# The first weight sum of each mix round: two fetches on GpSimd's queue in place of an add on VectorE

## The chip, the cores and the metric

One core of one Trainium2 chip runs the kernel. The metric is the device time of one execution in microseconds. A change of about 0.2% is what the timed runs of this kernel can tell from none.

## What is computed

One layer of a streaming encoder with sequence length S = 512 and model width D = 1024, all in float32. The part that matters here is the branch gates: three of them, each S x D, made from the normalised input and 3 x 1024 columns of w_in, then used to mix three branch results.

```python
h = rms_norm(x, attn_norm[l])
proj = h @ w_in[l]
q, k, v, f_logit, u, cv, cb, cc, g = jnp.split(proj, IN_SPLIT_POINTS, axis=-1)
...
y_a = forgetting_attention(...) @ w_proj_attn[l]
y_b = multiscale_pool(u, pool_w[l], pool_scale[l]) @ w_proj_pool[l]
y_c = short_gated_conv(cv, cb, cc, conv_w[l]) @ w_proj_conv[l]
gates = jax.nn.sigmoid(g + b_gate[l]).reshape(B, S, N_BRANCH, D)
mixed = gates[..., 0, :] * y_a + gates[..., 1, :] * y_b + gates[..., 2, :] * y_c
x = x + mixed @ w_out[l]
```

Then follow a SwiGLU block and a last norm.

## The kernel before

The kernel is written by hand, engine by engine, with semaphores between them. SyncE (SP) issues the loads, ScalarE rounds each weight block to a high part (whi), VectorE subtracts it to get the low part (wlo), and TensorE makes each product from three multiplies: high by high, high by low, low by high. TensorE takes float32 words of reduced precision at full speed, so each part is of that type. Weight blocks pass through rings: raw (three slots of 1024 columns, filled by SP), whi and wlo.

Its stages in order are norm, front, pair (four times), mix, rounds, out, ffn_first, ffn (three times), ffn_last and down. The change is in the rounds and in what prepares the first of them at the end of mix.

There are ten rounds (ROUNDS). Each makes two blocks of 128 gate columns of one branch, and the two blocks of that branch's projection. The gate product has a 2 x 2 block form: two column blocks by two halves of the model width (rows), and two halves of the tokens. It is computed in seven multiplications in place of eight, by sums of weight quarters and sums of token quarters. The weight quarters, each 128 x 512 in the tile, are b11 and b21 (load 0 of the round, first and second half of the rows for the first column block) and b12 and b22 (load 1, the same for the second block). Nine parts of weights go through the rings in a round: B11, B21, PRJ_A, T2, T1, T3, B22, PRJ_B, T4. TensorE works in this order: quarter products B11 and B21, projection PRJ_A, quarters T2, T1, T3, B22, projection PRJ_B, quarter T4. PRJ_A and PRJ_B are products of 128 x 512 tiles (lines 894 to 896), the quarters of 128 x 256 (lines 856 to 860).

The weight sums are made by sum_weights(r) on VectorE (lines 1840 to 1849), four adds of 128 x 512:

- weight_sum(0) = b11 + b12, the first sum, which becomes part T1
- b12 = b12 + b22, in place in raw, which becomes part T3
- weight_sum(1) = weight_sum(0) + b22, the second sum, part T2
- weight_sum(2) = weight_sum(1) + b21, the third sum, part T4

Each raises weight_summed by one, four a round. The three sums live in tail_32, a tile of 2,560 columns of which the token sums of the mix stage (chunk_whole, chunk_sums, chunk_lo; lines 1801 to 1824) use the first 2,048, until sums_lo_done reaches 4.

VectorE's own order in the loop over r is: post(r - 1) (gates times projections, L1880, and adds onto the merged branches, L1886), T3 and B22 low parts of round r, bank add c11 (L1906), PRJ_B, merged_lo (L1565) after a third branch, T4, then sum_weights(r + 1), bank add c12_first (L1914), B11 and B21 of round r + 1, bank adds c22 (L1921) and c12_second (L1929), and PRJ_A, T2 and T1 of round r + 1 (all low parts are L1855). In round 0 the parts B11 and B21 of round 1 stand ahead of sum_weights(1). ScalarE's order is alike: the high parts are L1250, the sigmoids L1289, the copies of banks L1274. In rounds 1 and up, the second gate's sigmoid stands between T2's and T1's high parts, and waits for the last bank add of the round.

SP's loads of a round (L535) wait until the ring slot is written out: load 0 for B21's low part of the round before and for all of its weight sums, load 1 for B22's low part, load 2 (two projection blocks) for PRJ_B's. Each load is two transfers of 256 KB, in rows of 128 elements of 4 bytes.

GpSimd makes constants at the start, issues 16 small copies within SBUF during the pair stage (L653, L655), and at the end of the kernel raises the variances to the power -0.5 (L663). Between the two it waits.

TensorE's waits in a round are: the low part of each quarter, kept (the bank copied by ScalarE), posted(4 r + 1) ahead of B22, and y_free ahead of the two projections, which post(r - 1) raises by its two multiplies.

Of the kernel before, what the change touches and what calls it, by code (L numbers as in the profile page):

```python
# [19 lines left out]
ALU = mybir.AluOpType  # L20
# [6 lines left out]
P = 128  # L27
# [11 lines left out]
ROUNDS = [(0, 2)] + [(i, br) for i in range(1, 4) for br in range(3)]  # L39
# [71 lines left out]
def hybrid_block(nc, x, attn_norm, w_in, b_forget, b_gate, w_proj_attn, pool_w, pool_scale,  # L111
# [3 lines left out]
    S, D = x.shape  # L115
# [22 lines left out]
    with ExitStack() as ctx:  # L138
# [3 lines left out]
        def sem(name):  # L142
            return ctx.enter_context(nc.semaphore(name))
# [167 lines left out]
        def weight_part(r, j):  # L311

            return PARTS_AT + PER_ROUND * r + j
# [14 lines left out]

        def weight_sum(j):

            return tail_32[:, j * HALF:(j + 1) * HALF]

        def gate_at(r, m):

# [89 lines left out]
        kept, posted, gates = sem("kept"), sem("posted"), sem("gates")  # L424
        y_free, merged = sem("y_free"), sem("merged")
        x_again = sem("x_again")

        def landed_down(k):

# [23 lines left out]
        def _(sp):  # L453
            def load(stage, i, j, halves, width=P):

                n, s = unit(stage, i, j)
                if stage == "out" and j < SLOTS:
                    sp.wait_ge(w_lo, weight_part(len(ROUNDS) - 1, (B21, B22, PRJ_B)[j]) + 1)
                    if j == 0:
                        sp.wait_ge(weight_summed, 4 * len(ROUNDS))  # L460
                    sp.sem_inc(loads_begun, 1)
                elif not (stage == "front" and n < SLOTS):
                    sp.wait_ge(w_lo, n - SLOTS + 1)


                    sp.sem_inc(loads_begun, 1)
                for src, at in halves:
                    nb = src.shape[0] // P
                    dst = raw[:, s, at * width:(at + nb) * width].rearrange(
                        "p (k c) -> p k c", c=width)  # L470
                    sp.dma_start(dst, src.rearrange("(k p) c -> p k c", p=P)
                                 ).then_inc(landed[s], 16)
# [65 lines left out]
            for r, (i, br) in enumerate(ROUNDS):  # L538
                if r == 0:
                    sp.wait_ge(w_lo, PARTS_AT - 2)  # L540
                else:
                    sp.wait_ge(w_lo, weight_part(r - 1, B21) + 1)
                    sp.wait_ge(weight_summed, 4 * r)
                load_round(r, 0, gate_columns(br, 2 * i))
                sp.wait_ge(w_lo, PARTS_AT - 1 if r == 0 else weight_part(r - 1, B22) + 1)
                load_round(r, 1, gate_columns(br, 2 * i + 1))
                sp.wait_ge(w_lo, PARTS_AT if r == 0 else weight_part(r - 1, PRJ_B) + 1)
                load_round(r, 2, projections((br, 2 * i), (br, 2 * i + 1)))
# [63 lines left out]
        @block.gpsimd  # L612
        def _(pool):
            nc.gpsimd.memset(ident[:], 0.0).then_inc(consts, 1)
            nc.gpsimd.memset(mask[:], 0.0).then_inc(consts, 1)
            nc.gpsimd.memset(ones[:], 1.0).then_inc(consts, 1)
            pool.wait_ge(consts, 3)
            nc.gpsimd.affine_select(out=ident[:], in_=ident[:], compare_op=ALU.not_equal, fill=1.0,
                                    base=0, pattern=[[-1, P]], channel_multiplier=1
                                    ).then_inc(consts, 1)  # L620
            nc.gpsimd.iota(steps16[:], pattern=[[1, PAD]], base=1, channel_multiplier=0
                           ).then_inc(consts, 1)

            diag = mask[:, S - P:S]
            nc.gpsimd.affine_select(out=diag, in_=diag, compare_op=ALU.is_ge, fill=NEG_INF,
                                    base=0, pattern=[[-1, P]], channel_multiplier=1
                                    ).then_inc(consts, 1)

            begun = 0
            for tiles, first, fill in ((Q2, 0, -1.0), (K2, 2, 1.0)):
                for a in range(2):
                    rows = op(tiles[a])
                    nc.gpsimd.memset(rows.bitcast(F32), 0.0).then_inc(f_consts, 1)
                    begun += 1
                    for r in (first, first + 1):
                        pool.wait_ge(f_consts, begun)
                        nc.gpsimd.affine_select(out=rows, in_=rows.bitcast(F32),
                                                compare_op=ALU.not_equal, fill=fill,  # L640
                                                base=-((1 - a) * HD + r), pattern=[[0, S]],
                                                channel_multiplier=1).then_inc(f_consts, 1)
                        begun += 1
            assert begun == F_CONSTS
            pool.wait_ge(f_consts, F_CONSTS)
            pool.wait_ge(vector_tile, count("vector_tile", "front", 0, 2))
            for i in range(WB):
                if i > 0:
                    pool.wait_ge(full[6], count("full6", "pair", i - 1, 2))
                for a in range(2):  # L650
                    h, at = 2 * i + a, (1 - a) * HD
                    f_pair = big_y[h:h + F_LOW + 1:F_LOW, F_AT:F_AT + S]
                    pool.dma_start(op(Q2[a], S, slice(at + 2, at + 4)).bitcast(F32), f_pair  # L653
                                   ).then_inc(f_in, 16)
                    pool.dma_start(op(K2[a], S, slice(at, at + 2)).bitcast(F32), f_pair  # L655
                                   ).then_inc(f_in, 16)


            nc.gpsimd.memset(stat[:, MINUS_HALF:MINUS_HALF + 1], -0.5).then_inc(power, 1)
            pool.wait_ge(power, 1)  # L660
            for t in range(TB):
                pool.wait_ge(x2_var, t + 1)
                nc.gpsimd.tensor_tensor(stat[:, 12 + t:13 + t], stat[:, 4 + t:5 + t],  # L663
                                        stat[:, MINUS_HALF:MINUS_HALF + 1], ALU.pow
                                        ).then_inc(x2_rstd, 1)
# [417 lines left out]
        def _(act):  # L1083
# [173 lines left out]

            def sum_hi(r, j, c, done):

                act.wait_ge(weight_summed, 4 * r + done)  # L1260
                part_hi(r, j, weight_sum(c))

            def t3_hi(r):

                act.wait_ge(weight_summed, 4 * r + 2)
                raw_hi(r, T3, 1, 0, 2)

            TOK = S // 2
# [56 lines left out]
            chunk_hi(1)  # L1325
            gate(4, 5, 3, 1, 1)
            raw_hi(0, PRJ_A, 2, 0)
            sum_hi(0, T2, 1, 3)
            sum_hi(0, T1, 0, 1)

            for r in range(len(ROUNDS)):
                last = r == len(ROUNDS) - 1
                if r > 0:
                    last_gate(r - 1)
                slots_free(r)
                keep(r, B11, 0, 0)
                t3_hi(r)
                raw_hi(r, PRJ_B, 2, 1)
                first_gate(r)
                if r > 0 and ROUNDS[r - 1][1] == 2:  # L1340
                    merged_hi(r - 1, 0)
                    merged_hi(r - 1, 1)
                keep(r, T2, 1, 0)
                sum_hi(r, T4, 2, 4)
                if last:
                    split_hi("out", 0, 0)
                    keep(r, T3, 1, 1)
                    split_hi("out", 0, 1)
                    second_gates(r)
                else:  # L1350
                    raw_hi(r + 1, B11, 0, 0, 2)
                    keep(r, T3, 1, 1)
                    raw_hi(r + 1, PRJ_A, 2, 0)
                    sum_hi(r + 1, T2, 1, 3)
                    if r == 0:
                        sum_hi(r + 1, T1, 0, 1)
                        second_gates(r)
                    else:
                        second_gates(r)
                        sum_hi(r + 1, T1, 0, 1)  # L1360
            last_gate(len(ROUNDS) - 1)
            merged_hi(len(ROUNDS) - 1, 0)
            merged_hi(len(ROUNDS) - 1, 1)
# [172 lines left out]
        def _(dve):  # L1536
# [291 lines left out]
            def sum_weights(r):  # L1828
# [8 lines left out]
                    dve.wait_ge(sums_lo_done, 4)  # L1837
                else:
                    dve.wait_ge(w_lo, weight_part(r - 1, T1) + 1)
                nc.vector.tensor_tensor(weight_sum(0), b11, b12, ALU.add  # L1840
                                        ).then_inc(weight_summed, 1)
                nc.vector.tensor_tensor(b12, b12, b22, ALU.add).then_inc(weight_summed, 1)
                dve.wait_ge(weight_summed, 4 * r + 1)
                nc.vector.tensor_tensor(weight_sum(1), weight_sum(0), b22, ALU.add
                                        ).then_inc(weight_summed, 1)
                dve.wait_ge(weight_summed, 4 * r + 3)
                if r > 0:
                    dve.wait_ge(w_lo, weight_part(r - 1, T4) + 1)
                nc.vector.tensor_tensor(weight_sum(2), weight_sum(1), b21, ALU.add
# [513 lines left out]
```

## Time and profile before

| what | value |
|---|---|
| timed runs | 797.62, 797.9 and 798.65 us, median 797.9 |
| the profiled execution | 797.29 us, span 795.1 us |
| mean granted clock of TensorE | 0.997 of full speed |
| TensorE busy | 778.7 us, 98% of the span |
| VectorE busy | 561.0 us, 71% |
| ScalarE busy | 362.3 us, 46% |
| GpSimd busy | 21.0 us, 3% |
| moved by DMA | 83.44 MB, mean 105 GB/s |

Busy times are of one profiled execution and are counted within its span; the time of that execution is 2.2 us longer than the span. The rounds lie between about 240 and 395 us. A start time in a row is counted from the start of the span. In views that show DMA shares as digits, each digit is the busy share of 16 engines in tenths, in one fortieth of the window.

### The profile page before, as it was taken

The page shows a single profiled execution, that of the slowest core. Times are in us where ns is not written, and L with a number is a line of the kernel's source. Part 1 is how long each engine was busy: PE and PEld are TensorE (multiplying, and loading weights), DVE is VectorE, ACT ScalarE, POOL GpSimd, SP SyncE. Part 2 cuts the span into 40 slices and gives each one's busy share as a digit, 9 for nine tenths or more (in the row PEclk, how much of TensorE's full clock was granted, in tenths as well). Part 3 has the DMA queues.
Part 4 walks back from the last instruction along what each step waited for, and adds up shares of the span by engine and source line. Part 5 has one row for each costly group of instructions (what it writes and reads, how often), then busy time and mean ns, then how long its engine had stood idle before and what let it go on. Part 6 is the DMA issues. An engine that isn't in the chain of part 4 may idle for free.

```text
span 795.1 us, 11564 instructions
## 1 busy us (share of the span) xinstructions
PE 778.7 (98%) x3931; PEld 663.3 (83%) x3931; DVE 561.0 (71%) x877; ACT 362.3 (46%) x604; POOL 21.0 (3%) x43
## 2 busy tenths in 40 slices
PE   5999999999999999999999999999999999999996
PEld 4878888888889999999988888888888888887885
DVE  7878686868798778777643465454445456799997
ACT  7265555656444555555433532222222223556554
POOL 4011010100000000000000000000000000000001
PEclk9999999999999999999999999999999999999998
DMA  7423232323234343343452133333323332353432
GB/s 226 121 77 97 54 98 61 82 70 84 67 95 106 98 115 100 87 120 94 147 193 84 54 110 102 87 98 106 106 84 101 106 93 93 131 183 110 148 104 106
DMA packets 129257, 83.44 MB, mean 105 GB/s; under 512 B 5484, under 2 KB 118180, under 8 KB 129220
## 3 DMA queue, kind: packets, MB, share of 16 engines
q1 hardware_dynamic: 128708, 82.89, 35.6%
q8 instruction: 22, 0.36, 0.2%
q0 software_dynamic: 512, 0.07, 0.1%
q14 instruction: 15, 0.12, 0.0%
HBM read 80.77 MB, written 2.10 MB: 104 GB/s over the span
## 4 chain that ended last, share of the span: by engine, by line
PE 93%; DVE 4%; DMA 1%; issue 1%; ACT 1%; SPq 0%; POOLq 0%; POOL 0%; ACTq 0%; DVEq 0%
PE bank L686 18%; PE bank L690 18%; PE bank L688 18%; PE bank L860 4%; PE bank L858 4%; PE bank L856 4%; PE bank L1028 3%; PE bank L1030 3%; PE bank L1029 3%; PE bank L894 2%; PE bank L895 2%; PE bank L896 2%; PE bank L938 2%; PE bank L940 2%; PE bank L942 2%; PE bank L800 1%
## 5 line engine op out<-in xcount | busy, mean ns | idle before, releaser
L686 PE MATMUL bank<-operands,whi 128*128 128x512 f32 x624 | 244.7, 392 | 1.0 <-DVE operands L1567 1.0
L690 PE MATMUL bank<-operands,wlo 128*128 128x512 f32 x624 | 243.1, 390 | 0.0
L688 PE MATMUL bank<-operands,whi 128*128 128x512 f32 x624 | 242.9, 389 | 0.0
L1558 DVE TENSOR_TENSOR wlo<-raw,whi 128x1024 fp32r<-128x1024 f32 x86 | 105.2, 1224 | 75.7 <-ACT whi L1092 74.0
L686 PEld LDWEIGHTS bank<-operands,whi 128*128 128x128 f32 x624 | 117.2, 188 | 25.4 <-DVE wlo L1558 1.5
L690 PEld LDWEIGHTS bank<-operands,wlo 128*128 128x128 f32 x624 | 117.1, 188 | 24.7
L688 PEld LDWEIGHTS bank<-operands,whi 128*128 128x128 f32 x624 | 117.2, 188 | 24.1 <-issue 0.2
L1092 ACT CAST whi<-raw 128x1024 fp32r<-128x1024 f32 x86 | 89.8, 1046 | 48.9 <-PE bank L690 25.0
L1098 ACT ACTIVATE work<-work 128x512 f32<-128x512 f32 (+1 forms) x24 | 15.2, 632 | 82.3 <-DVE work L2063 80.3
L860 PE MATMUL bank<-sums_hi,wlo 128*128 128x256 f32 x160 | 45.3, 283 | 0.0
L858 PE MATMUL bank<-sums_lo,whi 128*128 128x256 f32 x160 | 45.3, 283 | 0.0
L856 PE MATMUL bank<-sums_hi,whi 128*128 128x256 f32 x160 | 45.2, 283 | 0.0
L1855 DVE TENSOR_TENSOR wlo<-raw,whi 128x1024 fp32r<-128x1024 f32 (+1 forms) x40 | 38.1, 952 | 5.5 <-ACT whi L1250 5.5
L1030 PE MATMUL bank<-whi,operands 128*128 128x512 f32 (+1 forms) x97 | 37.5, 387 | 0.0
L1250 ACT CAST whi<-raw 128x1024 fp32r<-128x1024 f32 (+1 forms) x40 | 33.4, 837 | 8.6 <-PE bank L860 5.6
L2068 DVE TENSOR_TENSOR work<-bank,big_y 128x512 f32<-128x512 f32 x22 | 15.2, 691 | 31.1 <-PE bank L690 31.1
L1855 DVE TENSOR_TENSOR wlo<-tail,whi 128x512 fp32r<-128x512 f32 x30 | 20.5, 690 | 23.4 <-ACT whi L1250 23.4
L2063 DVE TENSOR_TENSOR work<-bank,big_y 128x512 f32<-128x512 f32 x22 | 15.1, 688 | 29.1 <-PE bank L690 24.1
L1029 PE MATMUL bank<-wlo,operands 128*128 128x512 f32 (+1 forms) x91 | 35.2, 387 | 0.0
L1028 PE MATMUL bank<-whi,operands 128*128 128x512 f32 (+1 forms) x91 | 35.2, 387 | 0.0
L860 PE MATMUL bank<-operands,wlo 128*128 128x256 f32 x120 | 34.0, 283 | 0.0
L858 PE MATMUL bank<-operands,whi 128*128 128x256 f32 x120 | 34.0, 283 | 0.0
(253 smaller groups left out, 1393.6 us busy)
## 6 DMA issues: line engine op xcount, KB each, us to landing
raw<-in_w_in_dram SPq DMA_DIRECT2D x106, 256.0 KB, 3.2
raw<-in_w_gate_up_dram SPq DMA_DIRECT2D x88, 256.0 KB, 3.2
raw<-in_w_down_dram SPq DMA_DIRECT2D x55, 256.0 KB, 2.8
big_x<-in_x_dram SPq DMA_DIRECT2D x8, 512.0 KB, 4.3
raw<-in_w_out_dram SPq DMA_DIRECT2D x16, 256.0 KB, 3.2
raw<-in_w_proj_attn_dram SPq DMA_DIRECT2D x8, 256.0 KB, 4.1
raw<-in_w_proj_pool_dram SPq DMA_DIRECT2D x8, 256.0 KB, 4.0
raw<-in_w_proj_conv_dram SPq DMA_DIRECT2D x8, 256.0 KB, 4.0
```

The source lines that it names most:

```text
L686: nc.tensor.matmul(banks[b][:, 0:width], whi[:, s, w], op(hi + k * S), start=a, stop=False)
L688: nc.tensor.matmul(banks[b][:, 0:width], whi[:, s, w], op(lo + k * S), start=False, stop=False)
L690: mm = nc.tensor.matmul(banks[b][:, 0:width], wlo[:, s, w], op(hi + k * S), start=False, stop=z)
L856: nc.tensor.matmul(to, wh[:, w], xh, start=first and k == 0, stop=False, skip_group_check=not first)
L858: nc.tensor.matmul(to, wh[:, w], xl, start=False, stop=False, skip_group_check=not first)
L860: mm = nc.tensor.matmul(to, wl[:, w], xh, start=False, stop=k == 3, skip_group_check=not first)
L1028: nc.tensor.matmul(to, h, wh, start=first, stop=False, skip_group_check=onto)
L1029: nc.tensor.matmul(to, h, wl, start=False, stop=False, skip_group_check=onto)
L1030: return nc.tensor.matmul(to, l, wh, start=False, stop=last, skip_group_check=onto)
L1092: nc.scalar.copy(whi[:, s, :], raw[:, s, :]).then_inc(w_hi, 1)
L1558: nc.vector.tensor_tensor(wlo[:, s, :], raw[:, s, :], whi[:, s, :].bitcast(F32), ALU.subtract).then_inc(w_lo, 1)
L1855: nc.vector.tensor_tensor(part_at(wlo, r, j, n), src, part_at(whi, r, j, n).bitcast(F32), ALU.subtract).then_inc(w_lo, n)
```

## The change

The first sum is taken from VectorE and made by DMA. GpSimd's queue issues two transfers for each round, both from w_in in HBM: the first writes b11 into weight_sum(0), the second, issued when the first has landed, adds b12 onto it. They raise a new semaphore, first_sum_in, by 16 each, 32 a round. The first of a round is issued when the tile of the first sum is free: for round 0 when the first half of the token sums has its low parts, later when T1's low part of the round before is written and its weight sums are all made. VectorE's second sum, and ScalarE's high part of T1, wait for first_sum_in in place of the first add. weight_summed counts three a round in place of four, and all who wait for it are renumbered. weight_sum(0) moves to the last 512 columns of tail_32, which the token sums don't use.

```diff
@@ weight_sum
-            return tail_32[:, j * HALF:(j + 1) * HALF]
+            at = (4, 1, 2)[j] * HALF
+            return tail_32[:, at:at + HALF]
@@ SP, load("out") and the round loads
-                        sp.wait_ge(weight_summed, 4 * len(ROUNDS))
+                        sp.wait_ge(weight_summed, 3 * len(ROUNDS))
-                    sp.wait_ge(weight_summed, 4 * r)
+                    sp.wait_ge(weight_summed, 3 * r)
@@ GpSimd, after the copies of the pair stage
+            for r, (i, br) in enumerate(ROUNDS):
+                if r == 0:
+                    pool.wait_ge(sums_lo_done, 2)
+                else:
+                    pool.wait_ge(w_lo, weight_part(r - 1, T1) + 1)
+                    pool.wait_ge(weight_summed, 3 * r)
+                for m, op_ in ((0, ALU.bypass), (1, ALU.add)):
+                    if m == 1:
+                        pool.wait_ge(first_sum_in, 32 * r + 16)
+                    col = COL_G + br * D + (2 * i + m) * P
+                    pool.dma_start(weight_sum(0).rearrange("p (k c) -> p k c", c=P),
+                                   w_in[0:4 * P, col:col + P].rearrange("(k p) c -> p k c", p=P),
+                                   accum_op=op_).then_inc(first_sum_in, 16)
@@ ScalarE
             def sum_hi(r, j, c, done):
-                act.wait_ge(weight_summed, 4 * r + done)
+                if done == 0:
+                    act.wait_ge(first_sum_in, 32 * r + 32)
+                else:
+                    act.wait_ge(weight_summed, 3 * r + done)
                 part_hi(r, j, weight_sum(c))
...
-                        sum_hi(r + 1, T1, 0, 1)
+                        sum_hi(r + 1, T1, 0, 0)
@@ VectorE, sum_weights
-                nc.vector.tensor_tensor(weight_sum(0), b11, b12, ALU.add
-                                        ).then_inc(weight_summed, 1)
                 nc.vector.tensor_tensor(b12, b12, b22, ALU.add).then_inc(weight_summed, 1)
-                dve.wait_ge(weight_summed, 4 * r + 1)
+                dve.wait_ge(first_sum_in, 32 * r + 32)
                 nc.vector.tensor_tensor(weight_sum(1), weight_sum(0), b22, ALU.add
                                         ).then_inc(weight_summed, 1)
-                dve.wait_ge(weight_summed, 4 * r + 3)
+                dve.wait_ge(weight_summed, 3 * r + 2)
```

## Rows read from the trace of the kernel before

**Rows 1.** The page: TensorE's busy time, GpSimd's DMA queue, shares of the chain.
```profile
PE 778.7 (98%) x3931; PEld 663.3 (83%) x3931; DVE 561.0 (71%) x877; ACT 362.3 (46%) x604; POOL 21.0 (3%) x43
...
q0 software_dynamic: 512, 0.07, 0.1%
...
PE 93%; DVE 4%; DMA 1%; issue 1%; ACT 1%; SPq 0%; POOLq 0%; POOL 0%; ACTq 0%; DVEq 0%
```

**Rows 2.** Busy time of each engine by stretch; one round's length.
```profile
core 0: us, PE busy (x) PEld busy (x) DVE busy (x) ACT busy (x) POOL busy (x), PEclk, DMA share, GB/s
...
301.80:317.40 15.60, 15.60 (x111) 14.62 (x110) 13.11 (x22) 8.79 (x16) 0.00 (x0) 1.00 0.39 104
```

**Rows 3.** Waits, 238 to 395 us, the longest in total: total, times, longest.
```profile
DVE wlo L1855 <- ACT whi L1250: 28.9, 24, 2.9
```

**Rows 4.** Timeline of VectorE, round 5's sums: start, duration, line, tiles, idle before.
```profile
301.84 0.69 DVE L1855 TENSOR_TENSOR wlo<-tail,whi 128x512 fp32r<-128x512 f32 x1 [0.29 <-ACT whi L1250]
...
311.16 0.68 DVE L1840 TENSOR_TENSOR tail<-raw 128x512 f32<-128x512 f32 x1
311.76 0.69 DVE L1842 TENSOR_TENSOR raw<-raw 128x512 f32<-128x512 f32 x1
312.36 0.69 DVE L1844 TENSOR_TENSOR tail<-tail,raw 128x512 f32<-128x512 f32 x1
...
314.03 1.22 DVE L1855 TENSOR_TENSOR wlo<-raw,whi 128x1024 fp32r<-128x1024 f32 x1
...
317.40 0.69 DVE L1855 TENSOR_TENSOR wlo<-tail,whi 128x512 fp32r<-128x512 f32 x1 [0.29 <-ACT whi L1250]
318.63 0.69 DVE L1880 TENSOR_TENSOR work<-bank,work 128x512 f32<-128x512 f32 x1 [0.54 <-ACT work L1289]
```

**Rows 5.** Timeline of VectorE, the same places in rounds 0, 1 and 2.
```profile
223.94 2.36 DVE L1824 TENSOR_TENSOR sums_lo<-tail,sums_hi 128x1024 fp32r<-128x1024 f32 x2
...
241.79 0.69 DVE L1855 TENSOR_TENSOR wlo<-tail,whi 128x512 fp32r<-128x512 f32 x1
...
252.40 0.69 DVE L1844 TENSOR_TENSOR tail<-tail,raw 128x512 f32<-128x512 f32 x1
...
255.32 1.29 DVE L1855 TENSOR_TENSOR wlo<-tail,whi 128x512 fp32r<-128x512 f32 x2
...
265.68 0.69 DVE L1844 TENSOR_TENSOR tail<-tail,raw 128x512 f32<-128x512 f32 x1
```

**Rows 6.** Timeline of TensorE: first multiplies of B11 and PRJ_A, round 5.
```profile
317.92 0.28 PE L856 MATMUL bank<-operands,whi 128*128 128x256 f32 x1
...
320.80 0.40 PE L894 MATMUL bank<-operands,whi 128*128 128x512 f32 x1
```

**Rows 7.** Timeline of ScalarE after round 5's last bank add: the second gate's sigmoid.
```profile
315.94 0.73 ACT L1289 ACTIVATE work<-work,vecs 128x512 f32<-128x512 f32 x1 [1.32 <-DVE work L1929]
```

**Rows 8.** DMA issues of lines 655 (GpSimd) and 535 (SP): ns; then landings.
```profile
L655 POOL DMA_DIRECT2D operands<-big_y x8: 540/540/546, 54.1 to 146.6; - x8
...
DMA to landing us min/median/max: 1.6/1.6/1.7
...
L535 SPq DMA_DIRECT2D raw<-in_w_in_dram x36: 367/438/510, 241.3 to 369.5; - x36
...
DMA to landing us min/median/max: 2.9/3.4/6.1
```

**Rows 9.** DMA view of 306.5 to 312.5 us, four loads of a round.
```profile
DMA  0000000006936599999999999999999999821000
...
DMA packets 2112, 1.05 MB, mean 175 GB/s; under 512 B 64, under 2 KB 2112, under 8 KB 2112
```

**Rows 10.** DMA view of 302.6 to 312.4 us.
```profile
DMA  9600000000000000000004758999999999999410
```

**Rows 11.** VectorE's groups from 243 to 393 us: first and last of 16.
```profile
L1855 DVE TENSOR_TENSOR wlo<-raw,whi 128x1024 fp32r<-128x1024 f32 (+1 forms) x38 | 36.2, 952 | 5.5 <-ACT whi L1250 5.5
...
L1868 DVE TENSOR_TENSOR work<-work 128x512 f32<-128x512 f32 x1 | 0.7, 692 | 0.1
```

More of the change, by code:

```diff
@@ L426, in hybrid_block @@
         x_again = sem("x_again")
+        first_sum_in = sem("first_sum_in")
         def landed_down(k):
@@ L1258, in sum_hi @@
             def sum_hi(r, j, c, done):
-                act.wait_ge(weight_summed, 4 * r + done)
+                if done == 0:
+                    act.wait_ge(first_sum_in, 32 * r + 32)
+                else:
+                    act.wait_ge(weight_summed, 3 * r + done)
                 part_hi(r, j, weight_sum(c))
             def t3_hi(r):
-                act.wait_ge(weight_summed, 4 * r + 2)
+                act.wait_ge(weight_summed, 3 * r + 1)
                 raw_hi(r, T3, 1, 0, 2)
@@ L1327, in _ @@
             raw_hi(0, PRJ_A, 2, 0)
-            sum_hi(0, T2, 1, 3)
-            sum_hi(0, T1, 0, 1)
+            sum_hi(0, T2, 1, 2)
+            sum_hi(0, T1, 0, 0)
             for r in range(len(ROUNDS)):
@@ L1343, in _ @@
                 keep(r, T2, 1, 0)
-                sum_hi(r, T4, 2, 4)
+                sum_hi(r, T4, 2, 3)
                 if last:
@@ L1353, in _ @@
                     raw_hi(r + 1, PRJ_A, 2, 0)
-                    sum_hi(r + 1, T2, 1, 3)
+                    sum_hi(r + 1, T2, 1, 2)
                     if r == 0:
-                        sum_hi(r + 1, T1, 0, 1)
+                        sum_hi(r + 1, T1, 0, 0)
                         second_gates(r)
@@ L1359, in _ @@
                         second_gates(r)
-                        sum_hi(r + 1, T1, 0, 1)
+                        sum_hi(r + 1, T1, 0, 0)
             last_gate(len(ROUNDS) - 1)
```

## The prediction

> **What bounds the kernel now.** I read the page first. TensorE is busy 98% of the span and carries 93% of the chain that ended last [rows 1], so a change pays only where TensorE waits. The busy times by stretch then show the rounds, the stage the change is in: in a 15.6 us stretch TensorE is busy for all 15.60 us at the full granted clock (2.4 GHz), while VectorE works 13.1 us [rows 2]. The list of waits from 238 to 395 us has rows for VectorE and ScalarE as the waiting engines only, the longest of 28.9 us [rows 3]; none names TensorE as the waiting engine. So no time can be won in the rounds; the question is only whether the new path stays inside its margins.
>
> Those come from VectorE's order of time. A round takes (312.36 - 265.68) / 3 = 15.56 us [rows 4, 5]. Take round 5. Its weight sums are four adds of 0.6 us each: the first sum at 311.16 (the removed one), b12 + b22 at 311.76, the second sum, which reads the first, at 312.36, the third behind it. Then come B11's low part (ends 314.03 + 1.22 = 315.25), the bank adds, and T2's and T1's low parts, the last ending at 317.40 + 0.69 = 318.09 [rows 4].
>
> **What is removed.** Ten adds of 0.68 us (about 0.60 from start to start), all on VectorE under a busy TensorE [rows 2, 4]: worth 0, and this cover is gone only where TensorE would wait for VectorE. Time stays saved only if VectorE's next instructions came earlier and something waited for them. The second sum now waits for the fetch, and TensorE wants B11(5) only at 317.92 [rows 6], 2.67 us after it is ready.
>
> **What is added: a wait with a deadline.** The first sum of round r now comes from two fetches of 256 KB on GpSimd's queue, one after the other, each waited for. The first may start once T1's low part of round r - 1 is written, since ScalarE and VectorE still read the tile until then; the weight_summed count is met earlier. Call D the time from there to the second fetch landed. For round 5 the start is 301.84 + 0.69 = 302.53 and the old second sum began at 312.36: D up to 9.83 us keeps the old schedule, and the same holds for rounds 3 to 9. Round 1 has 252.40 - (241.79 + 0.69) = 9.92, round 2 has 265.68 - (255.32 + 1.29) = 9.07 [rows 5]. Round 0 starts after the first half of the token sums at 226.30 and has 13.5 us, not in question [rows 5].
>
> Behind VectorE's new wait stand sums two and three, B11, three bank adds, PRJ_A, T2, T1 and, in the next round, the post of the gates. From second sum to T1's end VectorE takes 318.09 - 312.36 = 5.73 us, including the detour through ScalarE (the gate's sigmoid waits for the last bank add, T1's cast stands behind it) [rows 4, 7]. So the new path is a loop: T1's end, D, 5.73 us, T1's end. It fits the period if D + 5.73 is at most 15.56. Where it doesn't, the lateness adds up round by round, and TensorE is hit when it exceeds the slack. The tightest use is the post: PRJ_A(5) starts at 320.80 [rows 6] and needs its first multiply, ended at 318.63 + 0.69 = 319.32 [rows 4], so 1.5 us to spare, plus 0.54 us that VectorE idled before it [rows 4]: 2.0 us. B11 has 2.67. Hence, with D over the margins, loss = (D - 9.92) + (D - 9.07) + 7 x (D - 9.83) - 2.0, where a first term below zero counts nothing. It is 0.2 us at D = 10.0, 1.5 at 10.15, 9.2 at 11, 18 at 12, 36 at 14.
>
> **How long is D?** The trace has no fetch of this size on GpSimd's queue and no adding one. From below: GpSimd's 4 KB copies land 1.6 us after issue [rows 8]; 256 KB more cost the engines a quarter of what four such loads took them [rows 9]: the digits of that row add up to some 23.5 slices of 0.15 us, 3.5 us, so 0.88 us a load; a fetch is then 2.5 us and two are 5.0. From above: GpSimd's 16 copies made 512 packets [rows 1], 32 each, in 0.54 us of its time, 17 ns a packet if all of it scaled; one load has 2112 / 4 = 528 packets [rows 9], so 8.9 us each plus 1.1 us to landing, D = 20 for both. I take neither: SP's loads have the same bytes, rows and source, and land in 2.9 to 6.1 us, median 3.4 [rows 8]. GpSimd's issue of 0.54 us against SP's 0.44 makes that 3.5 us for the first fetch, which meets idle engines: they rest from 303.1 to 307.7 us (slices of 0.245 us) [rows 10].
>
> The second fetch begins about 302.6 + 3.5 = 306.1. It must read the tile, add and write back; I cost that at two passes of the engines, 1.75 us instead of 0.88. And it collides: SP's next four transfers reach the engines at 307.7 [rows 10] and keep them full until 311.6 [rows 9]. Sharing them halves its rate, so from 307.6 (I allow 1.5 us from its issue to full speed, of the 2.9 that SP's shortest landing takes with 0.88 of moving [rows 8]) it takes up to 3.5 us, and 0.5 us to report: landed about 311.6, a leg of 5.5 us. D = 3.5 + 5.5 + 0.1 for the queue to wake = 9.1 us, inside 10.15 by 1.0 us and level with round 2's 9.07 (an overrun there of some tenths is within the 2.0).
>
> The Trainium skill (DMA: Bandwidth & Descriptors, Anatomy of one DMA) puts a GpSimd fetch at 2.0 us plus bytes over 436 GB/s; by it, as an estimate, two are 5.2 us. SP's loads here land at 2.9 us at best, above that, so the sum doesn't go by it. Collectives: The Full Stack (The bandwidth ceiling) says a reducing transfer runs at about half rate because it reads two sources; this agrees with my two passes, and no row here shows it.
>
> **The other parties.** SP's loads share the engines with the second fetch and may land up to 1.7 us later. b12 and b22 are in the first half of the four transfers that keep the engines busy from 307.7 to 311.6 [rows 9, 10], so they land at about 310.6, and are first read at 311.16; the first add that needs them can now move from 311.16 to 311.76 and costs nothing there, and the next 0.54 us are idle time before the post. So some 1.7 us are covered: 0. The projections' load is wanted by a cast that feeds PRJ_A at 320.80: 0. ScalarE's wait for T1's cast is now on the fetch, but T2's cast before it already needs the second sum, which needs the fetch: 0. SP's round loads wait for a count of three in place of four, raised by the same third sum. GpSimd does nothing else in the rounds; its next work, the powers of the last norm, is 400 us later. The moved tile avoids the token sums. Traffic grows by 5.2 MB on 83.4; the engines are busy for 0.39 of a round's stretch [rows 2], so there is room but for the collision.
>
> Sum: 797.29 us (this execution, span 795.1) - 0 + 0 = 797.3; the three timed runs have a median of 797.9, 0.6 above it, so I predict 797.9.
>
> **The rivals.**
> 1. Slower by the loop (28%). The adding fetch is served behind all of SP's loads, or is worth three passes, and lands 1 to 3 us later: D of 10.15 to 12. The point of decision is D = 10.15. Price at 11: 9.2 us, 807; at 12: 816. For: D would be only 1.0 us over my sum, and every part of the second leg is unseen. Against: it begins a microsecond and more before the crowd, and takes turns with SP's queue, as I assume.
> 2. Much slower by descriptors (13%). GpSimd's own work grows with the packets, or it is held up beside VectorE, busy 13.1 of 15.6 us: D from 12 to 20. At 14 the time is 834, at 20 some 888. For: 0.54 us for only 32 packets. Against: that 0.54 us hardly varies, 540 to 546 ns over eight [rows 8], like a fixed cost. SBUF — State Buffer (SBUF: two separate sides) of the Trainium skill warns that VectorE in a two-port mode keeps GpSimd from writing descriptors; the 16 groups of VectorE instructions in the rounds are all TENSOR_TENSOR [rows 11], which the page (Who interferes with whom) says has no such mode, so by it this rival is not helped.
> 3. Faster (3%). VectorE's 0.6 us a round would have to reach a waiting TensorE; 2 us would give 795.9. No wait of TensorE's in the rounds speaks for it.
> 4. The change doesn't relieve VectorE: the removed 6 us come back as idle time before the second sum. That is likely even in my forecast and costs nothing.
>
> **How the numbers follow.** D below 10.15: 56%, time 797.9, own range 797 to 799.5. Rival 1: 28%, 799.5 to 816. Rival 2: 13%. Faster: 3%. A measurement of this kernel can tell about 0.2%, 1.6 us, from no change, which is the loss at D = 10.15. Faster 0.03, same 0.56, slower 0.41. The range runs from 797.0 to 815.0: it leaves out rival 2, a sliver of rival 1 and the faster case, some 0.18.
>
> **What would show it.** Right: TensorE busy throughout the rounds, round period 15.56 us; GpSimd's fetch issues of about 0.5 to 1.5 us, landings near 3.5 and 5.5; VectorE idle before the second sum for up to 0.6 us, with the fetch as releaser. Wrong: second landings over 6.6 us, a period longer than 15.56, VectorE idle for microseconds at that add, TensorE waiting at L894 or at B11. If the first leg is long too, it is rival 2; if only the second, rival 1.

## The result, and the profile after

The changed kernel takes 804.1 us (median of 4 runs, 802.91 to 805.5) against 797.76 us (4 runs, 797.48 to 798.65) for the kernel before: 6.3 us slower, ratio 1.0078 with a 95% interval of 1.0057 to 1.0099. The forecast was no change; the range of 797 to 815 held the time. A second set of four runs of the same kernel, shown as an experiment below, gave 805.23 us (801.22 to 806.37), ratio 1.0082 [1.0055, 1.011].

From the page of the profiled execution (803.21 us, span 801.4 us) I show the lines that answer to [rows 1], and the group of the new transfers (tile and source, count, KB, median us from issue to landing):

```profile
PE 781.6 (98%) x3931; PEld 664.4 (83%) x3931; DVE 555.0 (69%) x867; ACT 358.6 (45%) x604; POOL 41.9 (5%) x63
...
q0 software_dynamic: 6592, 5.31, 4.0%
...
PE 85%; DMA 7%; DVE 4%; issue 2%; ACT 1%; POOLq 0%; POOL 0%; ACTq 0%; SPq 0%; DVEq 0%
...
tail<-in_w_in_dram POOLq DMA_DIRECT2D x20, 256.0 KB, 5.1
```

VectorE works 6.0 us less, which is the removed work, and the kernel got slower. The chain that ended last now holds 7% DMA where it held 1%, and TensorE's share fell from 93% to 85%. In the page's list by line 6% of the span is the new transfer alone.

Busy time by stretch, changed kernel, columns as in [rows 2]; the stretch is nearly all of the rounds:

```profile
242.00:393.00 151.00, 147.62 (x1003) 136.21 (x1003) 105.40 (x169) 71.91 (x127) 18.45 (x18) 1.00 0.56 130
```

Before, TensorE was busy for all 151.00 us of this stretch and issued 1049 multiplies in it; now it issues 1003. At 15.56 us for the 111 multiplies of a round, 46 fewer are 6.4 us, so the whole loss is in the rounds. Only 3.4 us of it show as idle time: a multiply of a quarter is drawn as 0.28 us long while they start 0.12 us apart, so a gap between two starts shows only in part. The list of waits of the changed kernel, 238 to 400 us, shows the new one (total, times, longest):

```profile
POOL tail L674 <- DVE wlo L1872: 99.2, 9, 12.6
POOL tail L674 <- DMA tail<-in_w_in_dram: 27.7, 9, 4.5
DVE tail L1861 <- DMA tail<-in_w_in_dram: 21.9, 8, 3.3
```

L1861 is the second sum (L1844 before), L1872 the low parts (L1855 before), L1897 the post's multiply (L1880 before). VectorE now idles 21.9 us before its second sum, in 8 of 10 rounds; [rows 4] had none there. The chain of the changed kernel in the middle of the rounds, 289 to 307 us, start, duration and what:

```profile
289.12 0.70 DVE wlo L1872
289.82 0.28 issue
290.10 3.34 DMA tail<-in_w_in_dram
293.44 0.29 issue
293.73 7.07 DMA tail<-in_w_in_dram
...
300.82 0.70 DVE tail L1861
...
302.58 1.13 DVE wlo L1872
303.71 0.34 DVE work L1938
304.04 0.34 DVE work L1946
...
305.04 0.61 ACT whi L1266
...
306.28 0.69 DVE work L1897
```

This is the loop of the prediction, link by link: T1's low part ends at 289.82, GpSimd's queue wakes after 0.28 us, the plain fetch lands after 3.34, the queue wakes again after 0.29, the adding fetch takes 7.07, then VectorE's second sum and the way back to T1 (5.55 us, 5.73 before, since most of the 0.29 us that VectorE idled before T1's low part in [rows 4] is gone). The path D, from T1's end to the second sum, is 300.82 - 289.82 = 11.0 us in this round; with 5.55 it makes 16.55, where the period was 15.56. VectorE's own row of that second sum names what it waited for:

```profile
300.82 0.69 DVE L1861 TENSOR_TENSOR tail<-tail,raw 128x512 f32<-128x512 f32 x1 [2.54 <-DMA tail<-in_w_in_dram]
```

TensorE meets the lateness at B11 (line 872) first, and shortly after at PRJ_A (line 910). The first two rows are from the timeline of the changed kernel, the last two from its list of waits, 238 to 400 us; they are all that names its multiplies there:

```profile
303.85 0.36 PE L872 MATMUL bank<-operands,whi 128*128 128x256 f32 x1 [0.36 <-DVE wlo L1872]
...
307.11 0.47 PE L910 MATMUL bank<-operands,whi 128*128 128x512 f32 x1 [0.15 <-DVE work L1897]
...
PE bank L872 <- DVE wlo L1872: 2.4, 4, 1.3
PE bank L910 <- DVE work L1897: 0.5, 3, 0.2
```

### The profile page after: what moved, and what is told of

Its sections match the earlier page's. It is cut to its first block, busy times and chain, and to the rows that moved or that the text cites. A ratio compares the mean times of both kernels' runs of the same rounds, so it can differ in the third digit from the quotient of the medians.

```text
span 801.4 us, 11583 instructions
## 1 busy us (share of the span) xinstructions
PE 781.6 (98%) x3931; PEld 664.4 (83%) x3931; DVE 555.0 (69%) x867; ACT 358.6 (45%) x604; POOL 41.9 (5%) x63
## 4 chain that ended last, share of the span: by engine, by line
PE 85%; DMA 7%; DVE 4%; issue 2%; ACT 1%; POOLq 0%; POOL 0%; ACTq 0%; SPq 0%; DVEq 0%
PE bank L702 18%; PE bank L706 18%; PE bank L704 18%; DMA tail<-in_w_in_dram 6%; PE bank L1044 4%; PE bank L1046 4%; PE bank L1045 4%; PE bank L958 2%; PE bank L954 2%; PE bank L956 2%; PE bank L876 2%; PE bank L874 2%; PE bank L872 2%; DVE wlo L1872 1%; PE bank L910 1%
## 5 line engine op out<-in xcount | busy, mean ns | idle before, releaser
L1872 DVE TENSOR_TENSOR wlo<-raw,whi 128x1024 fp32r<-128x1024 f32 (+1 forms) x40 | 38.0, 949 | 3.3 <-ACT whi L1266 3.3
L1046 PE MATMUL bank<-whi,operands 128*128 128x512 f32 (+1 forms) x97 | 37.5, 387 | 0.0
L872 PE MATMUL bank<-operands,whi 128*128 128x256 f32 x120 | 34.3, 286 | 2.5 <-DVE wlo L1872 2.4
L874 PE MATMUL bank<-operands,whi 128*128 128x256 f32 x120 | 33.9, 283 | 0.0
```

The lines of the kernel that those rows point to most:

```text
L872: nc.tensor.matmul(to, wh[:, w], xh, start=first and k == 0, stop=False, skip_group_check=not first)
L874: nc.tensor.matmul(to, wh[:, w], xl, start=False, stop=False, skip_group_check=not first)
L1046: return nc.tensor.matmul(to, l, wh, start=False, stop=last, skip_group_check=onto)
L1872: nc.vector.tensor_tensor(part_at(wlo, r, j, n), src, part_at(whi, r, j, n).bitcast(F32), ALU.subtract).then_inc(w_lo, n)
```

## The experiments

Each experiment was run beside the kernel before, in two sets, each on one chip. The first set has four of them (kernel before: 797.75 us, 33 runs). Two explanations of the loss compete in them. By the loop theory the two fetches and VectorE's way back to T1 last longer than a round, so lateness adds up. By the contention theory the fetches' traffic makes SP's loads late, and these hold the engines up.

**Two tiles for the first sum.** Only the time at which a round's fetches may start is changed; the fetches and the adding stay.

```diff
-            at = (4, 1, 2)[j] * HALF
+            at = ((4, 0)[r % 2], 1, 2)[j] * HALF
...
+                elif r == 1:
+                    pool.wait_ge(sums_lo_done, 4)
+                    pool.wait_ge(first_sum_in, 32)
                 else:
-                    pool.wait_ge(w_lo, weight_part(r - 1, T1) + 1)
-                    pool.wait_ge(weight_summed, 3 * r)
+                    pool.wait_ge(w_lo, weight_part(r - 2, T1) + 1)
+                    pool.wait_ge(first_sum_in, 32 * r)
```

> Two tiles for the first sum, used in turn: the fetches of round r may start once T1's low part of round r - 2 is written, a whole round (15.56 us) earlier; the fetches, their bytes and the adding stay. Loop theory (the wait for the tile puts both fetches, some 11 us in the changed kernel, on a loop with VectorE's 5.55 us, which lasts longer than the period of 15.56): the fetches have some 25 us, are landed long before the second sum, the rounds go back to 15.56 us and the time to 797.8 (797.4 to 798.8). Contention theory (the fetches' traffic makes SP's loads late, and these hold VectorE and ScalarE): the traffic is the same, the time stays near 803, at least above 801.

Measured: 797.57 us (797.03 to 798.56), ratio 0.9997 [0.9988, 1.0006]; span 795.5. The fetches are about as long as in the changed kernel, the adding one 6.0 to 7.0 us from round 3 on. The two issues of round 6's pair, a round earlier than they were (columns as in the timelines):

```profile
303.83 0.77 POOL L677 DMA_DIRECT2D tail<-in_w_in_dram  x1 [10.87 <-DVE wlo L1875]
307.50 1.28 POOL L677 DMA_DIRECT2D tail<-in_w_in_dram  x1 [2.90 <-DMA tail<-in_w_in_dram]
```

Shortly after, VectorE makes the second sum of round 5 (L1864 here), whose own pair was issued at 288.02 and 291.68, without idling for it:

```profile
311.91 0.69 DVE L1862 TENSOR_TENSOR raw<-raw 128x512 f32<-128x512 f32 x1
312.51 0.69 DVE L1864 TENSOR_TENSOR tail<-tail,raw 128x512 f32<-128x512 f32 x1
```

In no round does it wait for a fetch; it waits for SP's loads four times, 4.8 us in all, and TensorE has no wait from 238 to 400 us. So the whole loss is the wait for the fetch, and it goes when the fetch starts a round earlier. This version is level with the kernel before, not faster: VectorE's free time still reaches nobody.

**The fetches beside the kernel before, for nobody.** All four adds stay on VectorE; the 20 fetches go, with the same waits in front (weight_summed counted by four) and one more for the pair before, to 512 columns that nobody reads.

```diff
+                    pool.dma_start(tail_32[:, 4 * HALF:5 * HALF].rearrange("p (k c) -> p k c", c=P),
+                                   w_in[0:4 * P, col:col + P].rearrange("(k p) c -> p k c", p=P),
+                                   accum_op=op_).then_inc(first_sum_in, 16)
```

> The kernel before, all four adds on VectorE, and beside it the same 20 fetches at the same places of the rounds into 512 columns that nobody reads; no engine of the rounds waits for them. Loop theory: nothing is waited for, so 797.8, with at most 0.5 us from loads that land later. Contention theory: the traffic and GpSimd's descriptor work alone cost most of the 6.3 us, 802 to 804.

Measured: 797.56 us (796.81 to 799.13), ratio 0.9999 [0.999, 1.0009]. SP's loads do land later here, at up to 7.1 us after issue (6.1 in [rows 8]), and engines wait for them, in the list of waits from 238 to 400 us:

```profile
ACT whi L1267 <- DMA raw<-in_w_proj_pool_dram: 6.1, 3, 2.9
DVE tail L1857 <- DMA raw<-in_w_in_dram: 4.7, 4, 1.8
```

yet TensorE has not one wait in that stretch. The fetches' traffic alone therefore costs nothing here, and the contention theory is out as a cause by itself. The cover that the prediction counted for the loads (1.7 us) was enough: VectorE's longest wait for one is 1.8 us.

**No fetch and no add.** After round 0 nobody makes the first sum and nobody waits for it (T1, T2 and T4 of rounds 1 to 9 then use an old sum).

```diff
-            for r, (i, br) in enumerate(ROUNDS):
+            for r, (i, br) in enumerate(ROUNDS[:1]):
...
-                    act.wait_ge(first_sum_in, 32 * r + 32)
+                    act.wait_ge(first_sum_in, 32)
...
-                dve.wait_ge(first_sum_in, 32 * r + 32)
+                dve.wait_ge(first_sum_in, 32)
```

> The changed kernel with the fetches of round 0 only; in rounds 1 to 9 the first sum is made by nobody (the weights of T1, T2 and T4 of these rounds are then not the reference's) and nobody waits for it. It measures what the removed add was worth by itself. Prediction's view (VectorE's 0.6 us a round lie under a busy TensorE): 797.8, within 0.5. Rival (VectorE's earlier low parts reach TensorE somewhere): up to 2 us under the kernel before, 796.

Measured: 797.43 us (796.74 to 798.47), ratio 0.9998 [0.9988, 1.0007]. Nine of the ten adds are gone and nothing stands in their place: they are worth 0, to about 0.1%.

**The second fetch plain.** b12 overwrites b11, the sum is left out.

```diff
-                for m, op_ in ((0, ALU.bypass), (1, ALU.add)):
+                for m, op_ in ((0, ALU.bypass), (1, ALU.bypass)):
```

> The second fetch of each round is a plain one too, so b12 overwrites b11 and the first sum is left out. If the adding itself makes the second leg long (7.0 us against 3.3 for the first): the leg falls to some 4.3 us even with SP's loads beside it, the whole path from 11.0 to 8.3, and the time to 797.8. If the collision with SP's loads makes it long: the leg stays at 6 us or more and the time at 801 to 804.

Measured: 797.35 us (796.98 to 798.45), ratio 0.9997 [0.9988, 1.0007]. The second leg, still beside SP's loads, lands after 3.5 to 5.1 us, median 4.1, against 5.2 to 8.0, median 7.0, in the changed kernel (rounds 1 to 9). The path is 0.28 + 3.4 + 0.29 + 4.1 = 8.1 us, under the margins, and the loss is gone. VectorE has no wait for a fetch.

The second set has four more (kernel before: 797.13 us, 13 runs).

**Only the adding fetch.** From round 1 on only b12 is added, at the place of the first fetch, so into idle engines; b11 is left out.

```diff
-                for m, op_ in ((0, ALU.bypass), (1, ALU.add)):
-                    if m == 1:
-                        pool.wait_ge(first_sum_in, 32 * r + 16)
+                for m, op_ in (((0, ALU.bypass), (1, ALU.add)) if r == 0 else ((1, ALU.add),)):
+                    if r == 0 and m == 1:
+                        pool.wait_ge(first_sum_in, 16)
...
-                dve.wait_ge(first_sum_in, 32 * r + 32)
+                dve.wait_ge(first_sum_in, 16 * r + 32)
```

ScalarE's wait is changed in the same way.

> From round 1 on only the second, adding fetch of a round is issued, at the place of the first (b11 is left out, the first sum is b12 onto the old contents, so the gates of these rounds are not the reference's). It meets the engines in their idle stretch ahead of SP's loads. If the adding itself is the price, it lands about 5 us after issue, as round 0's did in the changed kernel (5.2), against 3.3 for the plain one. If only the collision is, it lands at 3.3 to 3.8. The path is at most 5.5 us in both cases, so the time is 797.8.

Measured: 797.11 us (796.49 to 797.9), ratio 0.9998 [0.9987, 1.0008]. The view of its GpSimd line, 240 to 400 us (nine adding fetches: issue in ns, then landing in us):

```profile
L674 POOL DMA_DIRECT2D tail<-in_w_in_dram x9: 1260/1263/1277, 242.3 to 365.3; - x9
...
DMA to landing us min/median/max: 4.4/4.5/4.8
```

The same view of the kernel with two plain fetches:

```profile
L674 POOL DMA_DIRECT2D tail<-in_w_in_dram x18: 747/747/749, 242.9 to 369.3; - x18
```

The legs of all kernels, median us from issue to landing:

| | engines idle | beside SP's four transfers |
|---|---|---|
| plain | 3.3 (changed kernel, first leg) | 4.1 (both plain, second leg) |
| adding | 4.5 (only the adding fetch) | 7.0 (changed kernel, second leg) |

Adding costs 1.2 us on idle engines; GpSimd's issue is 0.5 us of that longer (1.26 against 0.75 us). The collision costs the plain fetch 0.8 us and the adding one 2.5. Neither alone makes 7.0; together they do. My expectation that one of the two would be the cause was too simple. The medians hide two rounds of the changed kernel, 6 and 7, in which the first leg is the one that meets SP's loads: it takes 4.3 and 5.0 us there, and the adding one 5.2 and 5.5.

The DMA views show how. First the adding fetch alone (only the adding fetch, 302.9 to 307.9 us), then the changed kernel from 306.6 to 317.3 us with both fetches and SP's loads, then the kernel with two plain fetches from 307.1 to 311.6:

```profile
GB/s 0 0 0 0 0 0 0 0 0 0 0 0 0 0 0 0 37 29 53 82 106 123 147 176 152 160 180 184 188 180 152 90 49 8 0 0 0 0 0 0
...
q0 software_dynamic: 528, 0.26, 45.4%
```

```profile
GB/s 260 48 21 21 10 92 153 153 352 230 0 0 0 0 0 0 21 94 144 272 343 335 327 306 228 165 151 168 191 182 191 203 213 274 318 314 220 130 34 21
...
q1 hardware_dynamic: 2287, 1.13, 40.8%
q0 software_dynamic: 608, 0.52, 29.5%
```

```profile
q0 software_dynamic: 80, 0.26, 18.6%
```

Alone, the adding fetch has its first bytes 2.0 us after issue and moves 0.26 MB in 18 slices of 0.125 us, 2.2 us, at 188 GB/s at most. The plain fetch at the start of the changed kernel's row moves as much in five slices of 0.27 us, 1.3 us, at up to 352. The adding one is 528 packets, as many as one of SP's loads [rows 9]; a plain fetch of GpSimd's is 80.

In the changed kernel the rate falls from 340 to some 180 GB/s for about eight slices while both queues are in flight. The same view of 313.2 to 315.3 us, a stretch in which they are, splits it by queue; the second fence is that of two plain fetches from 309.6 to 310.3 us:

```profile
q0 software_dynamic: 409, 0.21, 82.4%
q1 hardware_dynamic: 345, 0.17, 39.4%
```

```profile
q0 software_dynamic: 56, 0.21, 80.1%
q1 hardware_dynamic: 78, 0.04, 18.8%
```

So the adding fetch isn't starved. It moves a little more than SP's queue, in about as many packets, and each of its packets takes about 1.8 times as long (82.4% over 409 against 39.4% over 345). The plain fetch also gets about as many packets as SP's, but each carries eight times the bytes (0.21 MB in 56 against 0.04 in 78), so it is through before SP's loads. Both fit queues that take turns by packet; that rule was read from these two stretches and not tried by itself. The adding fetch, issued at 310.16, has its first bytes 2.7 us later and not 2.0, then moves about 100 GB/s (0.21 MB in 2.1 us) where it reached 188 alone, and lands at 317.3. From 315.3 to 317.3 us its last 80 packets trail among 706 of SP's; why they come so late stays open.

**Three plain fetches.** b11, b11 again, then b12, all plain: a long path without any adding. The edit is the one of the next experiment with the last ALU.add as ALU.bypass (the sum is left out).

> Three plain fetches one after the other in each round (b11, b11 again, b12 over it; the sum is left out): no adding at all, and a path of 0.28 + 3.3 + 0.29 + 4.1 + 0.29 + 3.5 = 11.7 us. Loop theory: only the length of the path counts. Slip of round 1 1.8, of round 2 2.6, of rounds 3 to 9 seven times 1.9, less 0.18 a round for VectorE's shorter way back (5.55), less the slack of 2.0: some 14 us, 812 (808 to 815). Rival (the adding fetches disturb something else, the plain ones don't): 797.8 to 799.

Measured: 819.83 us (818.06 to 820.8), ratio 1.0281 [1.0261, 1.03]. The direction and the cause are as the loop theory has them, the size isn't: 22.7 us, not 14. Its paths are 11.8 to 13.3 us, mean 12.6 over rounds 2 to 9, where I had 11.7: the second leg lands after 4.9 us (median) and not 4.1, and the first after 4.1 and 4.6 in two rounds instead of 3.3. With its measured paths the loop's sum gives 22 us. So the loss needs no adding; a path that is too long is enough.

**A third fetch, then the adding one.** b11 is fetched a second time over itself, and then b12 is added, so nothing of the computation is left out.

```diff
-                for m, op_ in ((0, ALU.bypass), (1, ALU.add)):
-                    if m == 1:
-                        pool.wait_ge(first_sum_in, 32 * r + 16)
+                for n, (m, op_) in enumerate(((0, ALU.bypass), (0, ALU.bypass), (1, ALU.add))):
+                    if n > 0:
+                        pool.wait_ge(first_sum_in, 48 * r + 16 * n)
...
-                dve.wait_ge(first_sum_in, 32 * r + 32)
+                dve.wait_ge(first_sum_in, 48 * r + 48)
```

ScalarE's wait is changed in the same way.

> The changed kernel with b11 fetched twice before b12 is added: the path grows by a plain fetch and its wake, 3.6 us, perhaps less 1 us since the adding fetch then meets less of SP's loads. Loop theory: nine rounds pay it in full, 9 x 2.6 to 9 x 3.6 = 23 to 32 us over the changed kernel's 804, so 827 to 836, with a round period of 19 to 20 us and VectorE's idle time before the second sum grown by as much. Contention theory: half more traffic for half more loss, 807.

Measured: 831.59 us (830.51 to 832.73), ratio 1.0425 [1.0408, 1.0443]: inside the 827 to 836 of the loop theory, far from 807. One round of it, GpSimd's queue and VectorE's second sum:

```profile
377.87 0.77 POOL L674 DMA_DIRECT2D tail<-in_w_in_dram  x1 [9.17 <-DVE wlo L1872]
381.51 0.75 POOL L674 DMA_DIRECT2D tail<-in_w_in_dram  x1 [2.87 <-DMA tail<-in_w_in_dram]
387.49 1.29 POOL L674 DMA_DIRECT2D tail<-in_w_in_dram  x1 [5.24 <-DMA tail<-in_w_in_dram]
```

```profile
391.96 0.69 DVE L1861 TENSOR_TENSOR tail<-tail,raw 128x512 f32<-128x512 f32 x1 [3.78 <-DMA tail<-in_w_in_dram]
```

Here the last leg is 4.4 us, as on idle engines: SP's four transfers, issued from 381.2 on, are through by about 387, before the adding fetch has bytes to move.

**The changed kernel again.**

> The changed kernel itself once more, for a second profile: 803 to 805.5. Loop theory: what it loses over the kernel before is the sum, over the rounds, of its paths less the margins of 9.92, 9.07 and 9.83 us, less 0.18 a round, less 2.0; if its paths differ from the first profile's (mean 11.0 us), its time differs by as much.

Measured: 805.23 us, and its profiled execution 806.37, span 804.6. The table has the books of the loop from five profiles (mean D of rounds 2 to 9; lateness: start of round 9's second sum less its 374.60 before; loss: span less 795.1; difference: lateness less loss):

| kernel | mean D, rounds 2 to 9 | lateness | loss | difference |
|---|---|---|---|---|
| both fetches plain | 9.9 | 0.7 | 0.5 | 0.2 |
| changed | 11.0 | 8.6 | 6.3 | 2.3 |
| changed, second profile | 11.1 (round 1: 12.1) | 11.4 | 9.5 | 1.9 |
| three plain | 12.6 | 23.4 | 22.5 | 0.9 |
| third fetch, then adding | 14.1 | 37.5 | 35.8 | 1.7 |

D is counted here from T1's end to the second sum, so that of both plain has VectorE's own order in it. In the four profiles that are truly late the loss is the lateness less 0.9 to 2.3 us, where the prediction read a slack of 2.0 from the post and 2.67 from B11. For the changed kernel the sum over the rounds is 0.21 + 1.47 + 8.50 over the margins, less 7 x 0.18 for the shorter way back, 8.9. T1's end of round 0 comes 0.26 us earlier than before (242.22 against 242.48), which leaves the 8.6 measured. That this sum closes is arithmetic, since every D is a difference of the same start times; the evidence is in the waits that name the fetch, and in the loss that follows the lateness. The two profiles of one kernel differ by 3.2 us of span because their legs do (the adding leg takes 5.2 to 8.1 us): the fetch is on the path that ends last. The changed kernel's four runs here scatter over 5 us, the 46 of the kernel before in both sets over 2.5 (796.3 to 798.8).

## Why the prediction was wrong

**Which case it was.** Rival 1, the loop, given 28%; the forecast of no change had 56%. The rival's path and place stand, and its price roughly: VectorE idle at the second sum with the fetch as releaser, a longer period, TensorE waiting at B11 and at PRJ_A, the first leg short and the second long in most rounds. Its two reasons for a long second leg stand only in part. The adding fetch wasn't served behind all of SP's loads but beside them, and alone its bytes took 2.2 us, 2.5 passes of the prediction's 0.88 us.

**The step that failed** is the size of the second leg, the adding fetch: 5.5 us in the sum, 7.0 measured (median). Two terms of it were too small. On idle engines the prediction's terms give 1.5 to full speed + 1.75 of moving + 0.5 to report = 3.75 us, and the run shows 4.5, with first bytes after 2.0 us and 2.2 us of moving. The issue is part of the first: I took GpSimd's 0.54 us from its 4 KB copies, and it is 0.77 for a plain and 1.28 for an adding fetch of this size. Beside SP's loads I halved its rate, 1.75 us more; the collision cost 2.5, since the first bytes also came later and the last ones trailed. A smaller third term: the queue's wake is 0.28 us and comes twice, 0.57 where I had 0.1. Together D is 11.0 and not 9.1, and the point of decision, 10.15, lies between.

**What held.** The first leg: 3.3 us in most rounds for the 3.5 of the sum, but 4.3 and 5.0 in rounds 6 and 7, where it met SP's loads, which the sum didn't foresee. The removed adds: worth 0 (no fetch and no add, 797.43). SP's loads: later, covered (unused fetches, 797.56). The margins of 9.92, 9.07 and 9.83: the kernel with both fetches plain stays within them and loses nothing. The slack of 2.0 was 0.9 to 2.3. By the formula D = 11.0 costs 9.2 us; measured are 6.3 and, in the second profile, 9.5. The formula had no term for the shorter way back, 0.18 us a round, 1.3 in all, and took D as equal in all rounds; with the measured paths and that term it leaves 6.9. Two passes for the adding were somewhat low: its moving took 2.2 us where the plain fetch's took 1.3, at up to 188 GB/s against up to 352. Collectives: The Full Stack (The bandwidth ceiling) of the Trainium skill says of a reducing collective that it runs at about half the rate of a copying one, since it reads two sources; the peak rates here are near that, and that two reads are the reason no run here shows. By the fit of DMA: Bandwidth & Descriptors (Anatomy of one DMA) of the Trainium skill a fetch would take 2.6 us, as an estimate; the plain one takes 3.3 and the adding one 4.5 to 7.0, so here the measurement decides against it. One reading of the rows was slightly off and changes nothing: the digits of [rows 9] add up to 22.0 slices as they stand, 3.3 us, and not 23.5. Rival 2 is out: 528 packets are issued in 1.26 us, 80 in 0.75, 32 in 0.54, far from proportional.

**What the chances should have been.** The sum stood 1.0 us from the point of decision with the second leg made of terms that no row showed: an issue taken from a copy 64 times smaller, a wake, and a share of the engines. All three turned out longer. With a margin of 1.0 us on an unseen leg of 5.5 us, the rows gave no good reason to lean towards no change.

## What to carry to other kernels

A fetch that may start only when its tile is free, and whose result the same engine needs before it frees the tile again, is a loop: add every leg, each wake of the queue included, and the way back, and compare with the period, not with the mean share of the DMA engines. A second tile (here 2 KB per partition that lay unused in the rounds) takes it off the path, as long as the fetches fit into the round that it adds; here that turned 804 us into 797.6. And look at who waits before work is moved: here the work was taken from an engine under a TensorE that never waited for it, it was worth nothing, and the change had only its risks.

## What the runs showed of the hardware

An adding fetch of 256 KB in rows of 512 bytes costs more than a plain one on the same queue: 1.26 us to issue against 0.75, 528 packets against 80, 2.2 us of moving against 1.3, and 2.5 us of delay beside 1 MB of SP's loads against 0.8. Beside those loads both kinds get roughly one packet for each of SP's (409 to 345, 56 to 78). The granted clock of TensorE, 1.00 in the rounds before and in the changed kernel, was lower on average where TensorE's gaps grew. The rounds of three plain fetches, with one stretch of them at the lower level (0.50, 1.2 GHz), and the rounds of the third fetch:

```profile
240.00:412.00 172.00, 157.27 (x1042) 145.31 (x1041) 108.28 (x173) 74.94 (x132) 20.18 (x27) 0.97 0.48 134
...
275.60:278.90 3.30, 3.30 (x17) 3.20 (x16) 3.20 (x5) 2.21 (x5) 0.75 (x1) 0.50 0.64 170
```

```profile
240.00:430.00 190.00, 166.10 (x1067) 154.03 (x1066) 111.49 (x178) 78.15 (x135) 25.32 (x27) 0.94 0.51 123
```

TensorE idles 15 of 172 us and 24 of 190 us there; from 270.0 to 275.5 us, just ahead of the slow stretch shown, it was busy for 3.2 of 5.5 us. The loss still follows VectorE's lateness, with a difference of 0.9 and 1.7 us where the changed kernel has 1.9 and 2.3 at full clock. So the slower clock can't have cost much; that was not tried by itself.
